# A decoder layer on one core: four more column pairs by seven products, a depthwise convolution split into even and odd tokens, and small sine tables

## What is computed

```python
h = rmsnorm(x, ln_pre)
z = h @ w_in          # 1024 x 7424
(c_val, c_glu, c_gate, q, k, v, a_gate, g_conv, g_attn) = split_columns(z)
u  = c_val * sigmoid(c_glu)                      # branch A
c  = causal depthwise conv of u, 31 taps, + b_dw # per channel, over tokens
ya = (silu(layernorm(c)) @ w_pw * silu(c_gate)) @ w_br_conv
q, k = partial_rope(q), partial_rope(k)          # first 16 of 64 dims of a head
yb = (windowed attention(q, k, v, sinks) * silu(a_gate)) @ w_br_attn
m  = sigmoid(g_conv) * ya + sigmoid(g_attn) * yb
x  = x + rmsnorm(m @ w_out, ln_post)
x  = x + sigmoid(x @ w_ple_gate) * (p @ w_ple_proj)
```

## Time and profile before

| | |
|---|---|
| median of 3 runs | 1108.25 us (1107.93 to 1109.26) |
| the profiled execution | 1108.18 us, of which the span of instructions is 1106.4 us |
| PE busy | 1100.5 us, 99% of the span, 6040 matmuls |
| DVE, ACT, POOL busy | 915.8, 475.8, 303.4 us |
| DMA | 148.21 MB, mean 134 GB/s |

### The profile page before, as it was taken

One profiled execution on the slowest core, in us unless ns is written; L12 is line 12 of the kernel. 1 busy time (PEld: TensorE's weight loads), 2 busy tenths in 40 slices (PEclk: granted clock), 3 DMA queues, 4 the chain that ended last, 5 costly groups with the idle time before them and its releaser, 6 DMA issues.

```text
span 1106.4 us, 16062 instructions
## 1 busy us (share of the span) xinstructions
PE 1100.5 (99%) x6040; PEld 896.1 (81%) x6040; DVE 915.8 (83%) x1094; ACT 475.8 (43%) x895; POOL 303.4 (27%) x216
## 2 busy tenths in 40 slices
PE   9999999999999999999999999999999999999998
PEld 7888888888888888777777888888888888888887
DVE  5998999999999999998885888787768878466875
ACT  6633333343442412566674442443436426344332
POOL 1069788888756941310000000000000000000000
PEclk9999999999999999999999999999999999999999
DMA  9802231322233232677742111464544843344655
GB/s 343 354 1 76 79 112 39 114 76 77 77 114 125 67 71 71 172 206 209 174 135 77 41 55 40 131 218 143 183 136 136 312 143 120 95 129 139 193 187 190
DMA packets 49540, 148.21 MB, mean 134 GB/s; under 512 B 5536, under 2 KB 6304, under 8 KB 47424
## 3 DMA queue, kind: packets, MB, share of 16 engines
q1 hardware_dynamic: 35648, 92.77, 25.8%
q10 hardware_dynamic: 11520, 37.75, 9.9%
q0 software_dynamic: 2304, 16.78, 6.4%
HBM read 119.37 MB, written 41.94 MB: 146 GB/s over the span
## 4 chain that ended last, share of the span: by engine, by line
PE 93%; DVE 3%; DMA 2%; ACT 1%; SPq 1%; issue 0%; POOL 0%; DVEq 0%; ACTq 0%
PE psg L737 41%; PE psg L926 24%; PE psb L1169 11%; PE psg L1077 7%; PE psg L761 2%; PE psb L991 1%; PE psg L1048 1%; PE psg L1169 1%; DMA x_rows<-x_rows 1%; PE psg L790 1%; PE psg L1122 1%; PE psg L1009 1%; ACT probs L1534 1%; PE psg L1043 1%; PE psg L1193 1%
## 5 line engine op out<-in xcount | busy, mean ns | idle before, releaser
L2042 DVE SCALAR_TENSOR_TENSOR psb<-conv,cols,psb 128x1021 f32<-128x1021 f32 (+6 forms) x196 | 233.5, 1268 | 0.0
L1227 POOL TENSOR_TENSOR pair_w<-early_raw,pair_w 128x512 fp32r<-128x512 f32 x91 | 125.0, 1383 | 78.4 <-ACT pair_w L1422 78.3
L926 PE MATMUL psg<-early_hi,pair_w 128*128 128x512 f32 x448 | 138.0, 389 | 0.0
L1210 POOL TENSOR_TENSOR rstd<-mean_sq,expo 128x4 f32<-128x4 f32 x3 | 3.1, 1020 | 383.3 <-DVE mean_sq L1872 363.4
L1858 DVE TENSOR_TENSOR w_lo<-w_raw,w_hi 128x1024 fp32r<-128x1024 f32 x57 | 69.8, 1224 | 41.1 <-ACT w_hi L1335 37.8
L926 PE MATMUL psg<-h_hi,pair_w 128*128 128x512 f32 x336 | 103.5, 389 | 0.0
L737 PE MATMUL psg<-h_hi,w_hi 128*128 128x512 f32 x320 | 99.0, 390 | 0.0
L737 PE MATMUL psg<-h_lo,w_hi 128*128 128x512 f32 x320 | 98.6, 389 | 0.0
L737 PE MATMUL psg<-h_hi,w_lo 128*128 128x512 f32 x320 | 98.6, 389 | 0.0
L1422 ACT ACTIVATE pair_w<-early_raw 128x512 fp32r<-128x512 f32 x91 | 56.4, 627 | 98.0 <-POOL early_raw L1243 74.6
L926 PEld LDWEIGHTS psg<-early_hi,pair_w 128*128 128x128 f32 x448 | 84.1, 188 | 17.5
(11 more groups left out here) (339 smaller groups left out, 2529.2 us busy)
## 6 DMA issues: line engine op xcount, KB each, us to landing
w_raw<-weights SPq DMA_DIRECT2D x68, 512.0 KB, 3.6
gates<-ring ACTq DMA_DIRECT2D x24, 512.0 KB, 3.6
w_sums<-w_pairs POOLq DMA_DIRECT2D x12, 1024.0 KB, 7.8
ring<-gates ACTq DMA_DIRECT2D x24, 512.0 KB, 4.4
block_raw<-w_sums SPq DMA_DIRECT2D x32, 256.0 KB, 3.2
early_raw<-w_pairs SPq DMA_DIRECT2D x7, 1024.0 KB, 5.5
block_raw<-w_pairs SPq DMA_DIRECT2D x24, 256.0 KB, 3.6
early_raw<-w_pairs SPq DMA_DIRECT2D x7, 768.0 KB, 4.4
```

The lines of the kernel that those rows point to most:

```text
L926: mm = nc.tensor.matmul(bank, pair_w[:, at_w, w, k * P:(k + 1) * P], r[:, k, :], start=(not onto and k == 0 and m == 0), stop=(k == KP - 1 ...
L1227: nc.gpsimd.tensor_tensor(pair_w[:, at_w, 1, :], early_source(s, n), pair_w[:, at_w, 0, :].bitcast(F32), ALU.subtract).then_inc(early_spli ...
L2042: own.step(stt(dst, row[:, 0:S - shift], tap(shift), dst, ALU.mult, ALU.add))
```

## The change

The q columns except tiles 3 and 7 (three pairs, kind `QUERY`) and k with v (one pair, kind `KV`) join the list of pairs; two plain q tiles are left, in front of attention.

```diff
-K_TILE, V_TILE = 4, 5
-Q0 = 6
-C0 = 14
+Q0 = 4
+PLAIN_Q = (3, 7)
+C0 = 6
-EARLY += [(GATTN, i) for i in range(PAIRS)]
+EARLY += [(QUERY, i) for i in range(3)] + [(GATTN, i) for i in range(PAIRS)] + [(KV, 0)]
+OTHER_TAPS = {P1: 4, Q5: 4, P6: 3, P2: 4, P7: 3, Q3: 2, P4: 4}
+VAL_TAPS = {P1: 4, Q5: 3, P6: 3, P2: 3, P7: 1, Q3: 1, P4: 3}
```

```diff
-                onto = n in (P6, P7, Q3, P4)
+                onto = n in (P2, P6, P7, Q3, P4)
...
-                    pe.wait_ge(early_kept, kept_at(s, {P6: P1, P7: P6, Q3: Q5}[n]))
+                    pe.wait_ge(early_kept, kept_at(s, {P2: P1, P6: P1, P7: P6, Q3: Q5}[n]))
...
-                dst = {P1: kept[:, 0, :], P6: kept[:, 1, :], Q5: kept_q5[:]}[n]
+                dst = {P1: early_bank(s, P2), P6: kept[:, 1, :], Q5: kept_q5[:]}[n]
```

```diff
-                    for shift in range(3, TAPS):
-                        dst = sums_of[shift % 2][:, shift:]
-                        dve.wait_ge(vec, own.base + own.n - 1)
-                        own.step(stt(dst, row[:, 0:S - shift], tap(shift), dst, ALU.mult, ALU.add))
+                    rest = [chain for k in range(1, 14) for chain in (even_tap(k + 1), odd_tap(k), sum_tap(k))]
+                    rest += [even_tap(15), sum_tap(14), odd_tap(14), sum_tap(15)]
+                    for n, (acc, source, shift, weight) in enumerate(rest):
+                        dve.wait_ge(vec, own.base + own.n - (2 if n < 40 else 1))
+                        own.step(stt(acc[:, shift:], source[:, 0:HALF - shift], weight, acc[:, shift:], ALU.mult, ALU.add))
```

The angles are made once as 128 x 64 elements (`make_angles`, `finish_angles` on POOL and two sines on ACT, during pairs 2 to 5), stored to DRAM and loaded back as the two 128 x 1024 tables. The rows for the packs now come from `gates` in DRAM, where the pairs' rows are stored, and the six q tiles are loaded back whole into `qo`. SP's list between the last pair and attention:

```diff
             def unpack(n):
 
                 sp.wait_ge(rope_done, n + 1)
-                for j in range(3 * n, 3 * n + 3):
+                sp.wait_ge(q_loaded, 96)
+                for j in range(4 * n, 4 * n + 3):
...
+            sp.wait_ge(early_made, EARLY_PRODUCTS - 1)
...
+            for table, first, last in ((cos_t, 0, 1), (sin_t, 1, 3)):
+                count = 8 * (last - first)
+                sp.dma_start(table[:], rows_of_angles(first, last).to_broadcast([P // count, count, S])).then_inc(pos_loaded, 16)
+            for j in (0, 1, 2):
+                pack(j)
+            main_read(sp, len(EARLY) - 1)
+            for g in range(2):
+                sp.dma_start(packs[0][ROT * g:ROT * g + ROT, :], k_raw[g * HD:g * HD + ROT, :]).then_inc(packed[0], 16)
+            for j in (4, 5, 6):
+                pack(j)
             for g in range(2):
                 for half in range(2):
                     sp.dma_start(kdup[half * HD + ROT:(half + 1) * HD, g, :],
                                  k_raw[g * HD + ROT:(g + 1) * HD, :]).then_inc(k_dup, 16)
...
+            for j in (0, 1, 2, 4, 5, 6):
+                sp.dma_start(qo[:, j, :], GATES[:, 3 * KT + j, :]).then_inc(q_loaded, 16)
+            load_tile(C0)
+            sp.wait_ge(conv_done, KT)
+            sp.dma_start(mixed[:], CONST[:, 1, :]).then_inc(masks_loaded, 16)
             unpack(0)
...
             unpack(1)
+            load_tile(C0 + 1)
```

More of the change, by code:

```diff
@@ L955, in _ @@
             tile(Q0 // 2, 1, h_hi, h_lo)
-            pairs(Q0 + 2, C0, h_hi, h_lo)
             def scores(p, jp):
@@ L2024, in tap, with both @@
                         return cols[:, COL_TAPS + i * TAPS + PAD - shift:COL_TAPS + i * TAPS + PAD - shift + 1]
+                    def both(shift):
+                        return fir_taps[:, i, 15 - shift:16 - shift]
                     out = conv[:, i, :]
                     row = sums[:] if q == 0 else out
-                    sums_of = (conv_sums(0), conv_sums(1))
+                    even, odd = by_parity(row)
+                    out_even, out_odd = by_parity(out)
+                    of_even, of_odd, of_sum = (fir_bank(n) for n in range(3))
                     if q < 2:
@@ L2034, in conv_steps @@
                         dve.wait_ge(conv_done, q)
-                    own.step(nc.vector.tensor_scalar(sums_of[1][:, 1:], row[:, 0:S - 1], tap(1), col("b_dw", i), ALU.mult, ALU.add))
+                    own.wait()
+                    own.step(nc.vector.tensor_scalar(of_even[:, 1:], even[:, 0:HALF - 1], tap(2), col("b_dw", i), ALU.mult, ALU.add))
                     yield
-                    own.step(nc.vector.tensor_scalar(sums_of[0][:, 2:], row[:, 0:S - 2], tap(2), None, ALU.mult))
+                    own.step(nc.vector.tensor_scalar(of_odd, odd, tap(1), None, ALU.mult))
@@ new lines, in conv_steps, with even_tap, odd_tap, sum_tap @@
+                    own.wait()
+                    own.step(nc.vector.tensor_scalar(of_sum, fir_sum[:], both(0), two_b[:, i:i + 1], ALU.mult, ALU.add))
+                    yield
+                    def even_tap(k):
+                        return of_even, even, k, tap(2 * k)
+                    def odd_tap(k):
+                        return of_odd, odd, k, tap(2 * k + 1)
+                    def sum_tap(k):
+                        return of_sum, fir_sum[:], k, both(k)
+                    rest = [chain for k in range(1, 14) for chain in (even_tap(k + 1), odd_tap(k), sum_tap(k))]
@@ L2043, in conv_steps @@
+                    rest += [even_tap(15), sum_tap(14), odd_tap(14), sum_tap(15)]
+                    for n, (acc, source, shift, weight) in enumerate(rest):
+                        dve.wait_ge(vec, own.base + own.n - (2 if n < 40 else 1))
+                        own.step(stt(acc[:, shift:], source[:, 0:HALF - shift], weight, acc[:, shift:], ALU.mult, ALU.add))
                         yield
                     own.wait()
-                    own.step(nc.vector.tensor_scalar(out[:, 0:1], row[:, 0:1], tap(0), col("b_dw", i), ALU.mult, ALU.add))
@@ L2046, in conv_steps @@
-                    own.step(stt(out[:, 1:], row[:, 1:], tap(0), sums_of[1][:, 1:], ALU.mult, ALU.add))
+                    own.step(nc.vector.tensor_scalar(out_even[:, 0:1], even[:, 0:1], tap(0), col("b_dw", i), ALU.mult, ALU.add))
+                    own.step(stt(out_even[:, 1:], even[:, 1:], tap(0), of_even[:, 1:], ALU.mult, ALU.add))
                     yield
                     own.wait()
-                    nc.vector.tensor_tensor(out[:, 2:], out[:, 2:], sums_of[0][:, 2:], ALU.add).then_inc(conv_done, 1)
+                    own.step(nc.vector.tensor_tensor(out_odd, of_sum, out_even, ALU.subtract))
@@ L2050, in conv_steps @@
+                    yield
+                    own.wait()
+                    own.step(nc.vector.tensor_tensor(out_even[:, 1:], out_even[:, 1:], of_odd[:, 0:HALF - 1], ALU.add))
+                    yield
+                    own.wait()
+                    nc.vector.tensor_tensor(out_odd, out_odd, of_odd, ALU.subtract).then_inc(conv_done, 1)
                     yield
```

344 lines of the change are left out of this document (174 added, 170 removed).

## The result

The changed kernel takes 1111.54 us (median of 20 runs), the kernel before 1108.3 beside it. The ratio is 1.0025, with a 95% interval of 1.0018 to 1.0033: slower by a quarter of a per cent, where 1103.6 us was predicted. The profiled execution took 1111.12 us, its span is 1109.3.

What follows compares the result with a forecast made beforehand. PE bounds the kernel, busy 1100.5 of 1106.4 us. Of 10.9 us fewer matmuls, 6.4 remain after a 4.5 us wait at the seam, less a 1.8 us second wait: 1108.18 - 4.6 = 1103.6 us, range 1097.0 to 1109.0.

Steps and rivals of the forecast that it cites:

- PE's second wait: Ahead of `turn(0)`: C0 + 1 lands at about 449.8, exponentials could begin 2.1 us late, so PE waits 1.8 us.
- the edits at nothing: PSUM C11, pair order, extra ACT and POOL work, small angles: they fit into existing room and add nothing to the sum.
- The rival of a bound DVE: Beside the pairs: reading every second element costs DVE more and PE waits; some 1220 us at double element time; chance 0.08.
- the 10.9 us: PE's matmuls: eight plain tiles at 10.88 us become four pairs at 19.04, 10.9 us less.
- the whole gain arrives: Rival at the seam: reloads in by 431 and C0 + 1 rounded by 444, giving 1097.3 us; chance 0.13.
- the reload of the q tiles in the seam step: Ahead of attention: six q tiles, issued from 425.4, first landing 3.6 later, five more at 1.39 each, in at 436.0.
- The clock fell in the wait: Rival: PE's clock falls while idle 4.5 us; scores to `turn(0)` stretch by 5.0, 1.8 hidden, so 1106.8 us; chance 0.10.
- POOL's copies, priced at 1 us: Part of the rival that all is given back at the seam: POOL's DMAs delay the second unpacking; 1106.2 to 1110; 0.13.
- the 0.10 for "slower": Whole kernel: chance 0.10 that the measured time is slower, beyond the 1106.0 to 1110.5 us counted as the same.
- the 9.1 us of the rope in place: Rotations before the scores: k's rows at about 422, two ropes at 5.1, rope in place at 9.1, ending at 441.3.

Runs made afterwards that it cites:

- the kernel with all repairs: Changed kernel with plain tables, early reloads, C0 + 1 loaded behind C0, and POOL's first copy held until the first scores: 1097.78 us, ratio 0.9899 to the kernel before.
- with the rows spread: Changed kernel with each 16-row pack load going to 16 partitions spread over the pack instead of neighbours, for its time alone: 1111.31 us, ratio 1.0027.
- the first experiment: Changed kernel with the load of tile C0 + 1 directly behind that of C0, ahead of the first unpacking: 1112.2 us, ratio 1.0039.
- with POOL's copy held too: Changed kernel with C0 + 1 loaded behind C0 and POOL's first 1 MB copy held until the first scores: 1108.7 us, ratio 1.0005.
- plain tables: Changed kernel with sine and cosine tables stored in DRAM with all copies, so each seam load reads 128 different rows: 1109.59 us, ratio 1.0007.
- early reloads: Changed kernel with reloads of q tiles 0, 1, 2, 4, 5 and both tables issued inside the last pair, not behind its sixth product: 1107.97 us, ratio 1.0000.
- early reloads and plain tables together: Changed kernel with only these two edits, C0 + 1 last in the list and POOL's copy not held: 1099.88 us, ratio 0.9925.

## Why the prediction was wrong

It foresaw the stretch, both waits and what releases them, and missed the sum by 7.9 us. In the profile it is 7.3 (`turn(0)` at 463.32, summed 456.0): 5.1 from the last reload, and most of the rest from C0 + 1, which took 6.0 us to land where 3.9 were summed.

| step of the prediction | summed | measured |
|---|---|---|
| last pair ends / scores possible | 416.9 / 439.6 | 416.48 / 439.30 |
| `kdup` issued, reloads begin | 425.4 | 426.26 |
| last reload lands | 436.0 | 441.10 |
| first scores (8.1 later) | 444.1 | 449.27 |
| C0 + 1 issued / landed | 445.9 / 449.8 | 451.22 / 457.24 |
| PE's second wait | 1.8 | 2.25 |
| `turn(0)` | 460.63 - 4.6 = 456.0 | 463.32 |

**PE, DVE and the edits at nothing: right.** Pairs of 19.04 us, taps of 745 ns in the page (743 taken; 0.65 from start to start, as summed), no PE wait inside the pairs. The rival of a bound DVE is out. That the 10.9 us are there to be had is shown by the kernel with all repairs: 1097.78, beside 1097.3 for "the whole gain arrives".

**The term that failed is the reload of the q tiles in the seam step, 436.0 against 441.10.** It priced SP's issues one after another and took the DMA engines as free when the reloads were issued, so that the first would land 3.6 after its issue as a lone load does. The trace has the first reload at 434.44, 8.2 after its issue: 4.6 us of backlog, and 0.9 from SP's issues; the five others took 6.7 (6.95 summed). What stood in front was the sine table, which counted as one issue of 0.36 us in the sum and landed 6.1 behind the cosine table, and 18 issues of few rows. With the tables stored plain the backlog falls from 4.6 to 1.2 us, and with the rows spread it falls as far: it takes both. A rule had been at hand: the Trainium skill, DMA: Bandwidth & Descriptors, Rules for kernel authors, says that a leading broadcast of c copies with a step of 0 confines a DMA to at most c of the 16 engines. The sine table has 8 copies in front, and the trace agrees: the load ends in 8 completion records (424.56 to 424.68), that of the cosine table, with 16 copies in front, in 16 (418.13 to 418.54); and it landed 6.1 us behind the cosine table, 1.9 as a plain load (417.54 and 419.41). Whether the fewer engines make up all of that difference no run shows: the cosine load too was slower with its copies, 4.5 us from issue to landing instead of 3.3.

**The second wait was right in cause; that its size came close, 1.8 against 2.25, is luck.** C0 + 1 was issued 1.95 us behind the first scores (1.8 summed), but landed 6.0 after its issue instead of 3.9. That alone would have made the wait some 3.9 us; the lower clock, which kept PE at work for 1.68 longer, took the difference. What slowed the load is not separated: POOL's copies, the rows of the second unpacking and the next weight tile ran beside it. That removing the wait alone gains nothing is shown by the first experiment; with POOL's copy held too, 2.8 us come back.

**Two mechanisms that the prediction had as rivals came along with the forecast.** The clock fell in the wait. The Trainium skill, TensorE: Matmul & The Clock Gate, Part 1, says that an idle PE goes back to half rate, and the rows agree (0.50 behind PE's idle time from 439.30 on). The fall cost PE 1.68 us, where 5.0 were priced, with 1.8 of them hidden. In the changed kernel all of it was hidden, since C0 + 1 ended the second wait; it shows, at 1.8, only where C0 + 1 is early. And POOL's copies, priced at 1 us in the way of the second unpacking, decide whether the last `kdup` rows take 2.4 or 4 to 6 us in the kernels whose chain runs into them. Of the 0.10 for "slower" only 0.02 came from the seam (the rest was DVE's): too little, since a longer chain brings the longer wait, the lower clock and the collision together.

One reading was off without weight in the sum: the 9.1 us of the rope in place hold two operations beside POOL's work, 1.84 and 3.41 us; in the changed kernel the same rope took 6.2 (438.42 to 444.63).

Open: why SP's issues take 1.0 to 1.5 us now and then (at 420.09 and 424.96 in the changed kernel, and near these places in the others), and how the drain divides between the sine table and the few-row issues. Each was removed alone (plain tables, spread rows). Each time the first reload landed 4.8 us after its issue instead of 8.2, so the two gains don't add up. The last reload came in only 2.2 us earlier with plain tables and 0.4 with spread rows: SP issued the reloads no earlier (with spread rows 2.2 us later), and the five behind the first took 7.6 and 7.4 us instead of 6.7.

## What to carry to other kernels

A list of DMAs has two paces, the queue's issues and the drain of the engines behind them; sum both, and take the later. A share near 1 at a low rate (here 0.98 at 241 GB/s) says that the second one binds. Transfers that feed a wait belong where the engines stand still, as soon as their place is free, and a load that repeats a few rows can be worth storing in DRAM in full, as the sine table was here. Waits at a seam don't add up edit by edit: here no repair that was run alone took more than 0.35% off the changed kernel; early reloads and plain tables together took 1.0%, and all together 1.2%.

## What the runs showed of the hardware

- The clock can fall after PE has resumed: in the kernel with plain tables and early reloads PE stood still for 2.5 us until 441.46, and the fall is in the window behind that:

```profile
440.00:442.00 2.00, 0.54 (x9) 0.57 (x11) 0.00 (x0) 0.09 (x1) 0.00 (x0) 1.00 0.95 246
442.00:444.00 2.00, 2.00 (x15) 1.58 (x12) 1.67 (x3) 0.00 (x0) 0.88 (x1) 0.54 0.79 299
```

- In the kernel with early reloads a DVE `tensor_tensor` of two SBUF operands takes 3.25 us beside POOL's `w_lo` subtraction of 2.43 (438.81 to 441.24), and 1.22 without it. The same happens in the kernel with all repairs (433.25, 3.16 us), on the chain that PE waits for; the 1.9 us more than cover its last 1.0 us of wait.
- A 1 MB copy from DRAM to DRAM on POOL's queue, issued some tenths of a microsecond ahead, about doubles the landing time of a 64 KB transfer on SP's queue (from 2.4 to between 4.5 and 5.9 us in six kernels).
